# Who makes the low parts of the experts' weights: VectorE with GpSimd, or VectorE alone

## The chip, the cores and the metric

The kernel runs on one core of a Trainium2 chip, in one launch. The metric is the device time of one execution in microseconds; the median of three runs of the kernel before is 1285.52 us (1283.47 to 1285.62). The core has a matrix engine (TensorE, PE in the profile, its weight loads PEld), VectorE (DVE), ScalarE (ACT), GpSimd (POOL) and SyncE (SP), which here only issues the transfers of weights.

## The reference

A two-layer transformer trunk over 256 tokens of 1024 numbers in float32. Each layer is: norm, one projection to 2304 columns, windowed attention on some heads and gated retention on others, an output projection, a residual sum; then norm, a SwiGLU mixer, a residual sum. The mixer of layer 0 is dense, that of layer 1 picks two of eight experts per token:

```python
for l in range(DEPTH):
    h = rms_norm(x, ln_mix[l])
    proj = h @ w_in[l]                                   # 1024 x 2304
    ya, yr = window_sink_attention(...), gated_retention(...)
    x = x + concatenate([ya, yr]) @ w_out[l]             # 1024 x 1024
    h = rms_norm(x, ln_ffn[l])
    if l % 2 == 0: y = swiglu(h, ffn_w_gate, ffn_w_up, ffn_w_down)   # 1024 x 2816, 2816 x 1024
    else:          y = moe_swiglu(h, router_w, exp_w_gate, exp_w_up, exp_w_down)
    x = x + y
# moe_swiglu: for e in 8 experts: y += gates[:, e] * (silu(h @ w_gate[e]) * (h @ w_up[e])) @ w_down[e]
```

## The kernel before

Every weight matrix is streamed once from HBM. The stream is cut into units of 128 x 2048 floats (1 MB), and each unit into two pieces of 128 x 1024. The ring `raw` holds 11 units (`RING`), so 22 pieces. A product in float32 precision is put together from three fast products: each operand is split into a high part (rounded to fp32r) and a low part (the rest). For a weight piece p, ScalarE writes `w_hi` as a rounded copy of the raw piece (`high_part`, line 373, for the pieces ahead of the experts, and `high_part_e`, line 393, for the experts'), and then `w_lo = raw - w_hi` is made (`low_part`, line 382, and `low_part_e`, line 400). `w_hi` has 6 slots (`HIGHS`), `w_lo` 3 (`LOWS`). TensorE's `piece` (line 1142 for every matmul, through `mm`) first does hi x hi and lo x hi with the high part, and only then waits for the low part and does the last third of its matmuls with `w_lo`.

Pieces are numbered through. 118 of them (`FRONT_PIECES`) belong to what comes before the experts: mixing in layer 0 (26), the dense mixer (66), mixing in layer 1 (26, numbers 92 to 117). Then a loop runs over the experts, 8 turns with these inputs (`n_pass` is 1), of 66 pieces each (`FFN_PIECES`): 44 of gate and up together, 22 of down. In `before`, `by_pool(p)` gives each piece with p % 4 == 3 to GpSimd, in front and in the loop alike, and the other three of four to VectorE. Each of the two counts its low parts on a semaphore of its own (`lo_vec`, `lo_pool`).

The order on each engine is written out by hand, and each engine runs its own list in order:
- TensorE: for q in 0..65 the piece q; after q = 5, 9, ... 45 two transposes of the hidden block (line 1139); after q = 3 the eight matmuls that spread the last expert's output over the tokens (`spread_out`); after q = 56 the gather of the next expert's tokens.
- VectorE: low parts 0, 1 and 2 among the low parts of the gathered tokens (line 1047) and of the output (line 1059); then for each q: `add_output` at q = 3 (line 1067, four instructions), at q % 4 == 3 the gated product `hid_e` (line 1105), which waits for ScalarE's silu, which waits for TensorE's piece q; at q % 4 == 1 the low part `heT_lo` of the transposed hidden block (line 1110), which waits for ScalarE's `heT_hi` (line 788); and last, low part q + 3. Low part q + 3 waits until TensorE has used piece q, whose slot it takes.
- ScalarE: for each q its share of the same steps, and last high part q + 6.
- SyncE: the load of unit m waits until the low parts of both pieces of unit m - 11 are made, since it overwrites them (`load_expert`, waits at line 478, loads at 484 and 489).
- GpSimd: in the loop nothing but low parts. Ahead of it, in layer 1's mixing, also the rotary embedding (`rope`, lines 529 to 534).

Of the kernel before, what the change touches and what calls it, by code (L numbers as in the profile page):

```python
# [20 lines left out]
F32 = mybir.dt.float32  # L21
F32R = mybir.dt.float32r
I32 = mybir.dt.int32
ALU = mybir.AluOpType
# [18 lines left out]
N_EXPERTS = 8  # L43
# [7 lines left out]
RING = 11  # L51
HIGHS, LOWS = 6, 3
# [8 lines left out]
FFN_UNITS = GU_UNITS + DOWN_UNITS  # L61
FFN_PIECES = 2 * FFN_UNITS
# [4 lines left out]
FRONT_PIECES = 2 * FRONT_UNITS  # L67
# [16 lines left out]

def by_pool(p):

    return p % 4 == 3


def lows(p, first=0):  # L90

    if p < first:
        done = [-sum(by_pool(q) == b for q in range(p + 1, first)) for b in (False, True)]
    else:
        done = [sum(by_pool(q) == b for q in range(first, p + 1)) for b in (False, True)]
    return done


def constants():
# [55 lines left out]
def trunk(nc, x, ln_mix, w_in, w_out, rel_bias_table, sinks, ln_ffn, ffn_w_gate, ffn_w_up, ffn_w_down,  # L155
          router_w, exp_w_gate, exp_w_up, exp_w_down, ln_final, consts, buckets, out):
    with ExitStack() as ctx:
        def sb(name, shape, dt=F32):
            return ctx.enter_context(nc.sbuf_tensor(name, shape, dt))

        def sem(name):
            return ctx.enter_context(nc.semaphore(name))
# [3 lines left out]
        w_hi = sb("w_hi", [P, HIGHS, PIECE], F32R)  # L166
# [114 lines left out]
        lo_vec, lo_pool = sem("lo_vec"), sem("lo_pool")  # L281
# [57 lines left out]
        for m in range(FFN_UNITS):  # L339
            e_total[e_slot[m]] += 32 if m < GU_UNITS else 16  # L340
            e_landed.append(e_total[e_slot[m]])
        lows_front = lows(FRONT_PIECES - 1)
        lows_e = lows(FFN_PIECES - 1)

        def wait_lows(eng, p, lead=(0, 0), first=0):

            b = by_pool(p)
            eng.wait_ge((lo_vec, lo_pool)[b], lead[b] + lows(p, first)[b])

        assert FRONT_PIECES % 4 == FFN_PIECES % 4 and FFN_UNITS % RING == 0  # L350
        assert FFN_PIECES % HIGHS == 0 and FFN_PIECES % LOWS == 0

        def high_slot(p):
# [6 lines left out]
        def raw_piece(slot, half):  # L360
            return raw[:, slot, half * PIECE:(half + 1) * PIECE]
# [30 lines left out]
            act.wait_ge(piece_used, FFN_PIECES * i + (FRONT_PIECES + q - HIGHS + 1))  # L392
            nc.scalar.activation(w_hi[:, q % HIGHS, :], raw_piece(slot, q % 2), ACT.Copy).then_inc(hi_made, 1)  # L393

        def low_part_e(eng, i, q, pool):
            if q >= FFN_PIECES or by_pool(q) != pool:
                return
            eng.wait_ge(hi_made, FFN_PIECES * i + (FRONT_PIECES + q + 1))
            eng.wait_ge(piece_used, FFN_PIECES * i + (FRONT_PIECES + q - LOWS + 1))
            eng.tensor_tensor(w_lo[:, q % LOWS, :], raw_piece(e_slot[q // 2], q % 2),  # L400
                              w_hi[:, q % HIGHS, :].bitcast(F32), ALU.subtract).then_inc((lo_vec, lo_pool)[pool], 1)

        block = ctx.enter_context(nc.Block())

# [2 lines left out]
        def _(sp):  # L407
# [56 lines left out]
            def load_expert(i, e):  # L464
                for m in range(FFN_UNITS):
                    slot = e_slot[m]
                    freed = []
                    for half in range(2):
                        q = 2 * (m - RING) + half
                        b = by_pool(q % FFN_PIECES)  # L470
                        if q >= 0:
                            rel = lows(q)[b]
                        else:
                            rel = lows(FFN_PIECES + q, FFN_PIECES)[b]
                        freed.append(((lo_vec, lo_pool)[b], sp.to_reg(lows_e[b] * i + (lows_front[b] + rel))))

                    for s, value in freed:
                        sp.wait_ge(s, value)
                    if m < GU_UNITS:
                        j, hf = m // 2, m % 2  # L480
                        dst = raw[:, slot, :].rearrange("p (k g n) -> p k g n", k=4, g=2)
                        for g, w in enumerate((exp_w_gate, exp_w_up)):
                            src = w[0, bass.ds(e, 1), hf * 4 * P:(hf + 1) * 4 * P, j * FC:(j + 1) * FC]
                            sp.dma_start(dst[:, :, g, :], src.rearrange("e (k p) n -> p (e k) n", p=P)).then_inc(raw_landed[slot], 16)
                    else:
                        u = m - GU_UNITS
                        dst = raw[:, slot, :].rearrange("p (k n) -> p k n", k=2)
                        src = exp_w_down[0, bass.ds(e, 1), u * 2 * P:(u + 1) * 2 * P, :]
                        sp.dma_start(dst, src.rearrange("e (k p) n -> p (e k) n", p=P)).then_inc(raw_landed[slot], 16)
# [5 lines left out]
            n = sp.value_load(passes_i[0:1, 0:1], min_val=1, max_val=2)  # L495
# [15 lines left out]
        def _(pool):  # L511
# [28 lines left out]
            first = 0  # L540
# [36 lines left out]
            pool.dma_start(gain[:], ln_final.partition_broadcast(P)).then_inc(gain_landed, 16)  # L577
            pool.wait_ge(route_ready, 1)
            n = pool.value_load(passes_i[0:1, 0:1], min_val=1, max_val=2)
            with pool.Fori(0, n * N_EXPERTS) as i:  # L580
                for q in range(FFN_PIECES):
                    low_part_e(pool, i, q, True)

            pool.wait_ge(gain_landed, 32)
            pool.wait_ge(x_added, n * (4 * N_EXPERTS) + 14)
# [224 lines left out]
        def _(dve):  # L810
# [44 lines left out]
            first = 0  # L855
            for layer in range(DEPTH):
                n = 2 * layer
# [119 lines left out]
                n = 1  # L977
# [67 lines left out]
            def gather_low(i, b):  # L1045
                dve.wait_ge(g_hi, 2 * i + (b + 1))
                dve.tensor_tensor(aT_lo[:, 4 * b:4 * b + 4, 0:P], bank(2 + b).rearrange("p (k t) -> p k t", k=4),
                                  aT_hi[:, 4 * b:4 * b + 4, 0:P].bitcast(F32), ALU.subtract).then_inc(g_lo, 1)

            def rstd_low(i):  # L1050
                dve.wait_ge(rstd_gathered, i + 1)
                dve.tensor_copy(rstd_e[:], psum[:, 5, 300:301]).then_inc(rstd_e_made, 1)
# [35 lines left out]
            dve.wait_ge(route_ready, 1)  # L1088
            n_pass = dve.value_load(passes_i[0:1, 0:1], min_val=1, max_val=2)
            with dve.Fori(0, n_pass * N_EXPERTS) as i:  # L1090
                low_part_e(dve, i, 0, False)
                gather_low(i, 0)
                low_part_e(dve, i, 1, False)
                gather_low(i, 1)
                rstd_low(i)
                for q in range(2, LOWS):
                    low_part_e(dve, i, q, False)
                output_low(i)
                for q in range(FFN_PIECES):
                    j = q // 4  # L1100
                    if q == 3:
                        add_output(i)
                    if q < GU_PIECES and q % 4 == 3:
                        dve.wait_ge(e_gate, NJ * i + (j + 1))
                        dve.scalar_tensor_tensor(out=hid_e[:, j % 2, :], in0=psum[:, j % 2, FC:2 * FC], scalar=rstd_e[:],  # L1105
                                                 in1=hid_e[:, j % 2, :], op0=ALU.mult, op1=ALU.mult).then_inc(e_hid, 1)
                    if q % 4 == 1 and 1 <= j <= NJ:
                        dve.wait_ge(e_hi, NJ * i + j)
                        cols = slice(2 * (j - 1), 2 * j)
                        dve.tensor_tensor(heT_lo[:, cols, :], psum[:, 4 + (j - 1) % 2, 0:256].rearrange("p (k t) -> p k t", k=2),  # L1110
                                          heT_hi[:, cols, :].bitcast(F32), ALU.subtract).then_inc(e_lo, 1)
                    if q == 48:

                        dve.wait_ge(pick_turned, i + 1)
                        mark_slots(i + 1)
                    low_part_e(dve, i, q + LOWS, False)
            turns = n_pass * N_EXPERTS
            output_low(turns)
            add_output(turns)
# [17 lines left out]
        def _(pe):  # L1137
# [24 lines left out]
            def piece(p, products, i=None, each=False, tiles=None):  # L1162

                r = p if i is not None else p - FRONT_PIECES
                high, low = w_hi[:, r % HIGHS, :], w_lo[:, r % LOWS, :]
                if i is None:
                    pe.wait_ge(hi_made, p + 1)  # L1170
                else:
                    pe.wait_ge(hi_made, FFN_PIECES * i + (FRONT_PIECES + p + 1))
                for n, (dst, hi, lo, cols, start, stop) in enumerate(products):
                    if tiles:
                        pe.wait_ge(h_hi, tiles[n])
                        pe.wait_ge(h_lo, tiles[n])
                    mm(dst, hi, high[:, cols], start, False)
                    mm(dst, lo, high[:, cols], False, False)
                if i is None:
                    wait_lows(pe, p)  # L1180
                else:
                    b = by_pool(p)
                    pe.wait_ge((lo_vec, lo_pool)[b], lows_e[b] * i + (lows_front[b] + lows(p)[b]))
                for n, (dst, hi, lo, cols, start, stop) in enumerate(products):
                    ins = mm(dst, hi, low[:, cols], False, stop)
                    if each and n < len(products) - 1:
                        ins.then_inc(product_out, 1)
                ins.then_inc(piece_used, 1)

            pe.wait_ge(i_landed, 16)  # L1190
            first = 0
            for layer in range(DEPTH):
                turn_h(2 * layer)
                for s in range(MIX_PIECES):
                    if s < IN_PIECES:
                        u, half = s // 2, s % 2
# [309 lines left out]
```

## Time and profile before

| what | us |
|---|---|
| median of three runs | 1285.52 |
| span of the profiled execution, first to last instruction | 1282.0 |
| PE matmul busy | 1211.1 (94%) |
| DVE busy | 950.1 (74%) |
| ACT busy | 849.9 (66%) |
| POOL busy | 468.4 (37%) |
| DMA, mean over the span | 268 GB/s |

The profile gives for its own execution the span alone; the median of the runs is 3.5 us above it. The times are inclusive of all stages: the front takes up to about 420 us, the eight turns of the expert loop the rest. Busy shares are means over stages, and a matmul's span overlaps the next one's, so where TensorE loses time is read from the starts of its instructions, not from its busy share. "Idle before" is the time for which an engine stood still ahead of an instruction, and behind the arrow is what it waited for.

### The profile page before, as it was taken

To read this page: it belongs to the slowest core of one execution; us is meant where nothing else is said; L and a number is where in the kernel's file an instruction comes from. 1 tells how busy PE (TensorE), PEld (TensorE's weight loads), DVE (VectorE), ACT (ScalarE), POOL (GpSimd) and SP (SyncE) were. 2 spreads that over 40 slices of the span, in tenths; PEclk is the share of its full clock that TensorE was granted. 3 is DMA by queue.
4 is the path that set the end of the run, shared out by engine and by line. 5 is a ranking of instruction groups with operands and counts; after the bars stand their busy time and mean duration, and the time that the engine had idled before them with its cause. 6 is when DMAs were issued, how large, how long until landed. Compare 5 with 4: busy or idle time off the path is not lost.

```text
span 1282.0 us, 20404 instructions
## 1 busy us (share of the span) xinstructions
PE 1211.1 (94%) x6173; PEld 1001.2 (78%) x6173; DVE 950.1 (74%) x1031; ACT 849.9 (66%) x1108; POOL 468.4 (37%) x204
## 2 busy tenths in 40 slices
PE   7899999999897999999999999999999999999996
PEld 7887888888895877777877777777787777777775
DVE  4765444435766788788788798888978878878885
ACT  6655444435553787677777677778777767768773
POOL 2402211222414254344344444435434534443542
PEclk9999999999998899999999999999999999999999
DMA  9945555565343599999999999999999999999950
GB/s 284 359 134 174 187 197 190 172 191 170 99 150 114 176 349 341 315 329 330 327 322 346 316 315 346 341 301 342 338 316 326 341 316 324 346 341 293 348 197 33
DMA packets 259816, 344.06 MB, mean 268 GB/s; under 512 B 8672, under 2 KB 231088, under 8 KB 259776
## 3 DMA queue, kind: packets, MB, share of 16 engines
q1 hardware_dynamic: 259200, 342.35, 80.4%
q0 software_dynamic: 352, 1.09, 0.3%
q8 instruction: 24, 0.39, 0.1%
q10 hardware_dynamic: 224, 0.10, 0.0%
q14 instruction: 16, 0.13, 0.0%
HBM read 342.06 MB, written 1.44 MB: 268 GB/s over the span
## 4 chain that ended last, share of the span: by engine, by line
PE 67%; DVE 18%; issue 9%; ACT 4%; DMA 2%; DVEq 1%; SPq 0%; ACTq 0%
PE psum L1142 64%; DVE w_lo L400 11%; PE psum L1139 3%; DMA raw<-in_w_in 1%; ACT w_hi L393 1%; DVE x_sb L1067 1%; DVE hid_e L1105 1%; ACT score L666 1%; DVE prob L922 1%; DVE oe_lo L1059 1%; ACT heT_hi L788 1%; ACT aT_hi L758 1%; DVE rt L1020 0%; DVE esink L911 0%; DVE smax L907 0%
## 5 line engine op out<-in xcount | busy, mean ns | idle before, releaser
L400 DVE TENSOR_TENSOR w_lo<-raw,w_hi 128x1024 fp32r<-128x1024 f32 x400 | 599.4, 1528 | 65.5 <-PE psum L1142 63.0
L393 ACT ACTIVATE w_hi<-raw 128x1024 fp32r<-128x1024 f32 x528 | 549.9, 1059 | 131.3 <-PE psum L1142 128.0
L400 POOL TENSOR_TENSOR w_lo<-raw,w_hi 128x1024 fp32r<-128x1024 f32 x128 | 360.8, 2819 | 490.8 <-PE psum L1142 426.1
L1142 PE MATMUL psum<-w_hi,aT_hi 128*128 128x512 f32 (+1 forms) x1232 | 451.6, 375 | 3.3 <-ACT proj L653 2.0
L1142 PE MATMUL psum<-w_hi,aT_lo 128*128 128x512 f32 (+1 forms) x1232 | 442.4, 368 | 0.0
L1142 PE MATMUL psum<-w_lo,aT_hi 128*128 128x512 f32 (+1 forms) x1232 | 326.9, 369 | 25.4 <-DVE w_lo L400 25.4
L1142 PEld LDWEIGHTS psum<-w_lo,aT_hi 128*128 128x128 f32 x1232 | 213.6, 190 | 72.6 <-DVE w_lo L400 35.8
L1142 PEld LDWEIGHTS psum<-w_hi,aT_hi 128*128 128x128 f32 x1232 | 234.3, 190 | 41.4 <-ACT proj L653 2.5
L1142 PEld LDWEIGHTS psum<-w_hi,aT_lo 128*128 128x128 f32 x1232 | 234.3, 190 | 35.0
L373 ACT ACTIVATE w_hi<-raw 128x1024 fp32r<-128x1024 f32 x118 | 124.0, 1058 | 84.0 <-PE psum L1142 75.5
L382 POOL TENSOR_TENSOR w_lo<-raw,w_hi 128x1024 fp32r<-128x1024 f32 x29 | 71.4, 2461 | 260.2 <-PE psum L1142 235.6
L382 DVE TENSOR_TENSOR w_lo<-raw,w_hi 128x1024 fp32r<-128x1024 f32 x89 | 113.4, 1276 | 47.9 <-PE psum L1142 45.9
L1142 PE MATMUL psum<-w_hi,heT_hi 128*128 128x512 f32 x352 | 140.6, 399 | 0.0
L1142 PE MATMUL psum<-w_hi,heT_lo 128*128 128x512 f32 x352 | 139.1, 395 | 0.0
L1142 PE MATMUL psum<-w_lo,heT_hi 128*128 128x512 f32 x352 | 111.6, 398 | 8.8 <-DVE w_lo L400 8.8
L1142 PEld LDWEIGHTS psum<-w_lo,heT_hi 128*128 128x128 f32 x352 | 65.3, 188 | 27.7 <-DVE w_lo L400 12.5
L1110 DVE TENSOR_TENSOR heT_lo<-psum,heT_hi 128x256 fp32r<-128x256 f32 x88 | 36.9, 420 | 61.5 <-ACT heT_hi L788 61.5
L1142 PEld LDWEIGHTS psum<-w_hi,heT_lo 128*128 128x128 f32 x352 | 66.2, 188 | 15.2
L1142 PEld LDWEIGHTS psum<-w_hi,heT_hi 128*128 128x128 f32 x352 | 66.1, 188 | 15.3
L788 ACT ACTIVATE heT_hi<-psum 128x256 fp32r<-128x256 f32 x88 | 33.8, 384 | 47.1 <-PE psum L1139 47.1
L785 ACT ACTIVATE hid_e<-psum,rstd_e 128x256 f32<-128x256 f32 x88 | 41.8, 475 | 28.5 <-PE psum L1142 28.5
L1105 DVE SCALAR_TENSOR_TENSOR hid_e<-psum,rstd_e,hid_e 128x256 f32<-128x256 f32 x88 | 41.9, 476 | 2.7
(188 smaller groups left out, 843.7 us busy)
## 6 DMA issues: line engine op xcount, KB each, us to landing
raw<-in_exp_w_gate SPq DMA_DIRECT2D x176, 512.0 KB, 4.7
raw<-in_exp_w_up SPq DMA_DIRECT2D x176, 512.0 KB, 5.8
raw<-in_exp_w_down SPq DMA_DIRECT2D x88, 1024.0 KB, 6.5
raw<-in_w_in SPq DMA_DIRECT2D x17, 1024.0 KB, 5.4
raw<-in_ffn_w_gate SPq DMA_DIRECT2D x22, 512.0 KB, 4.1
raw<-in_ffn_w_up SPq DMA_DIRECT2D x22, 512.0 KB, 5.1
raw<-in_ffn_w_down SPq DMA_DIRECT2D x11, 1024.0 KB, 4.9
raw<-in_w_out SPq DMA_DIRECT2D x8, 1024.0 KB, 8.0
```

Source lines behind the costliest of these rows:

```text
L373: nc.scalar.activation(high_slot(p), raw_piece((p // 2) % RING, p % 2), ACT.Copy).then_inc(hi_made, 1)
L382: eng.tensor_tensor(low_slot(p), raw_piece((p // 2) % RING, p % 2), high_slot(p).bitcast(F32), ALU.subtract).then_inc((lo_vec, lo_pool)[po ...
L393: nc.scalar.activation(w_hi[:, q % HIGHS, :], raw_piece(slot, q % 2), ACT.Copy).then_inc(hi_made, 1)
L400: eng.tensor_tensor(w_lo[:, q % LOWS, :], raw_piece(e_slot[q // 2], q % 2), w_hi[:, q % HIGHS, :].bitcast(F32), ALU.subtract).then_inc((lo ...
L666: nc.scalar.activation(score[:, c, p, :], score[:, c, p, :], ACT.Exp, bias=nmax[:, col:col + 1], accum_out=psums[:, col:col + 1]).then_inc ...
L758: nc.scalar.activation(aT_hi[:, 4 * b:4 * b + 4, 0:P], bank(2 + b).rearrange("p (k t) -> p k t", k=4), ACT.Copy).then_inc(g_hi, 1)
L785: nc.scalar.activation(hid_e[:, j % 2, :], psum[:, j % 2, 0:FC], ACT.Silu, scale=rstd_e[:]).then_inc(e_gate, 1)
L788: nc.scalar.activation(heT_hi[:, 2 * (j - 1):2 * j, :], psum[:, 4 + (j - 1) % 2, 0:256].rearrange("p (k t) -> p k t", k=2), ACT.Copy).then ...
L1105: dve.scalar_tensor_tensor(out=hid_e[:, j % 2, :], in0=psum[:, j % 2, FC:2 * FC], scalar=rstd_e[:], in1=hid_e[:, j % 2, :], op0=ALU.mult, ...
L1110: dve.tensor_tensor(heT_lo[:, cols, :], psum[:, 4 + (j - 1) % 2, 0:256].rearrange("p (k t) -> p k t", k=2), heT_hi[:, cols, :].bitcast(F32 ...
L1139: return pe.matmul(dst, src, ident, is_transpose=True, start=True, stop=True, skip_group_check=True)
L1142: return pe.matmul(dst, a, b, start=start, stop=stop, skip_group_check=True)
```

## The change

GpSimd makes no low part of an expert's piece any more, nor of the 22 pieces that lie ahead of these in the ring (numbers 96 to 117). VectorE makes them, at the same places of its list by the same rule (low part q + 3 at step q). The other pieces of the front stay divided as they were. With one semaphore for the expert's low parts, the waits of SyncE and of TensorE become simpler: SyncE waits once, for the second piece of the unit, in place of twice. GpSimd's loop over the experts goes.

```diff
 def by_pool(p):
-    return p % 4 == 3
-def lows(p, first=0):
-    ...
+    return p % 4 == 3 and p < FRONT_PIECES - 2 * RING
+def lows(p):
+    return [sum(by_pool(q) == b for q in range(p + 1)) for b in (False, True)]

-        def low_part_e(eng, i, q, pool):
-            if q >= FFN_PIECES or by_pool(q) != pool:
+        def low_part_e(eng, i, q):
+            if q >= FFN_PIECES:
                 return
             eng.wait_ge(hi_made, FFN_PIECES * i + (FRONT_PIECES + q + 1))
             eng.wait_ge(piece_used, FFN_PIECES * i + (FRONT_PIECES + q - LOWS + 1))
             eng.tensor_tensor(w_lo[:, q % LOWS, :], raw_piece(e_slot[q // 2], q % 2),
-                              w_hi[...].bitcast(F32), ALU.subtract).then_inc((lo_vec, lo_pool)[pool], 1)
+                              w_hi[...].bitcast(F32), ALU.subtract).then_inc(lo_vec, 1)

             def load_expert(i, e):
-                    freed = [...]              # one wait for each of the unit's two pieces
-                    for s, value in freed:
-                        sp.wait_ge(s, value)
+                    q = 2 * (m - RING) + 1
+                    sp.wait_ge(lo_vec, FFN_PIECES * i + (lows_front[0] + q + 1))

         # GpSimd
-            with pool.Fori(0, n * N_EXPERTS) as i:
-                for q in range(FFN_PIECES):
-                    low_part_e(pool, i, q, True)

         # VectorE, for each low part of the loop
-                    low_part_e(dve, i, q + LOWS, False)
+                    low_part_e(dve, i, q + LOWS)

         # TensorE, ahead of the last third of a piece
-                    b = by_pool(p)
-                    pe.wait_ge((lo_vec, lo_pool)[b], lows_e[b] * i + (lows_front[b] + lows(p)[b]))
+                    pe.wait_ge(lo_vec, FFN_PIECES * i + (lows_front[0] + p + 1))
```

## Rows read from the trace of the kernel before

**Rows 1.** Waits, whole span: engine and line waited for; us, times, longest us.

```profile
DVE heT_lo L1110 <- ACT heT_hi L788: 61.5, 57, 1.2
...
PE psum L1142 <- DVE w_lo L400: 34.2, 32, 1.4
```

**Rows 2.** The page's part 5: groups (busy, mean ns | idle before, releaser).

```profile
L400 DVE TENSOR_TENSOR w_lo<-raw,w_hi 128x1024 fp32r<-128x1024 f32 x400 | 599.4, 1528 | 65.5 <-PE psum L1142 63.0
...
L400 POOL TENSOR_TENSOR w_lo<-raw,w_hi 128x1024 fp32r<-128x1024 f32 x128 | 360.8, 2819 | 490.8 <-PE psum L1142 426.1
```

**Rows 3.** Line 400: its instructions, ns min/median/max.

```profile
L400 DVE TENSOR_TENSOR w_lo<-raw,w_hi x400: 1204/1214/3447, 419.7 to 1265.7; 128x1024 fp32r<-128x1024 f32 x134
```

**Rows 4.** Timeline of PE, second turn: start us, us, engine, line, what [idle before].

```profile
542.19 0.44 PE L1139 MATMUL psum<-cst,hid_e 128*128 128x128 f32 x2
...
549.17 0.38 PE L1139 MATMUL psum<-cst,hid_e 128*128 128x128 f32 x2
...
560.78 0.38 PE L1139 MATMUL psum<-cst,hid_e 128*128 128x128 f32 x2
...
566.52 0.38 PE L1139 MATMUL psum<-cst,hid_e 128*128 128x128 f32 x2
...
568.94 0.73 PE L1142 MATMUL psum<-w_lo,aT_hi 128*128 128x512 f32 x2 [1.12 <-DVE w_lo L400]
...
570.89 0.39 PE L1142 MATMUL psum<-w_hi,aT_hi 128*128 128x512 f32 x1
...
573.62 0.38 PE L1139 MATMUL psum<-cst,hid_e 128*128 128x128 f32 x2
...
647.43 0.43 PE L1139 MATMUL psum<-cst,hid_e 128*128 128x128 f32 x2
```

**Rows 5.** Timeline of POOL and DVE around that stall.

```profile
565.40 2.40 POOL L400 TENSOR_TENSOR w_lo<-raw,w_hi 128x1024 fp32r<-128x1024 f32 x1 [2.34 <-ACT w_hi L393]
...
565.59 3.29 DVE L400 TENSOR_TENSOR w_lo<-raw,w_hi 128x1024 fp32r<-128x1024 f32 x1
...
568.81 0.41 DVE L1110 TENSOR_TENSOR heT_lo<-psum,heT_hi 128x256 fp32r<-128x256 f32 x1
569.14 2.35 DVE L400 TENSOR_TENSOR w_lo<-raw,w_hi 128x1024 fp32r<-128x1024 f32 x2
571.60 0.48 DVE L1105 SCALAR_TENSOR_TENSOR hid_e<-psum,rstd_e,hid_e 128x256 f32<-128x256 f32 x1
...
574.45 0.42 DVE L1110 TENSOR_TENSOR heT_lo<-psum,heT_hi 128x256 fp32r<-128x256 f32 x1 [1.23 <-ACT heT_hi L788]
```

**Rows 6.** Timeline of PE, same turn, pieces of down.

```profile
603.82 0.48 PE L1142 MATMUL psum<-w_hi,heT_hi 128*128 128x512 f32 x1
...
606.64 0.40 PE L1142 MATMUL psum<-w_hi,heT_hi 128*128 128x512 f32 x1
...
608.04 0.40 PE L1142 MATMUL psum<-w_hi,heT_hi 128*128 128x512 f32 x1
```

**Rows 7.** Windows: stretch, busy by engine, PEclk, DMA share, GB/s.

```profile
30.00:40.00 10.00, 9.29 (x79) 9.09 (x79) 4.40 (x8) 4.92 (x8) 2.31 (x2) 1.00 1.10 348
...
45.00:50.00 5.00, 5.00 (x44) 5.00 (x44) 4.90 (x5) 0.47 (x3) 3.50 (x3) 1.00 1.03 409
...
545.00:650.00 105.00, 100.81 (x465) 81.39 (x464) 89.33 (x84) 79.38 (x95) 45.08 (x16) 1.00 1.00 330
```

**Rows 8.** Timeline of DVE and PE where the second turn begins.

```profile
535.66 3.37 DVE L400 TENSOR_TENSOR w_lo<-raw,w_hi 128x1024 fp32r<-128x1024 f32 x2
...
537.02 0.62 PE L1142 MATMUL psum<-w_lo,aT_hi 128*128 128x512 f32 x2
...
538.95 2.72 DVE L1067 SCALAR_TENSOR_TENSOR x_sb<-psum,gatex,x_sb 128x512 f32<-128x512 f32 x4
```

**Rows 9.** Timeline of PE in layer 1's mixing.

```profile
350.86 3.62 PE L1139 MATMUL psum<-cst,prob 128*128 128x128 f32 x16 [3.22 <-DVE prob L922]
```

**Rows 10.** The page's part 6: loads, count, KB each, median us to landing.

```profile
raw<-in_exp_w_down SPq DMA_DIRECT2D x88, 1024.0 KB, 6.5
```

More of the change, by code:

```diff
@@ L85, in by_pool @@
 def by_pool(p):
-    return p % 4 == 3
-def lows(p, first=0):
[L92 to L96, printed above, removed]
+    return p % 4 == 3 and p < FRONT_PIECES - 2 * RING
+def lows(p):
+    return [sum(by_pool(q) == b for q in range(p + 1)) for b in (False, True)]
 def constants():
@@ L342, in trunk, with wait_lows @@
         lows_front = lows(FRONT_PIECES - 1)
-        lows_e = lows(FFN_PIECES - 1)
-        def wait_lows(eng, p, lead=(0, 0), first=0):
+        def wait_lows(eng, p):
             b = by_pool(p)
-            eng.wait_ge((lo_vec, lo_pool)[b], lead[b] + lows(p, first)[b])
-        assert FRONT_PIECES % 4 == FFN_PIECES % 4 and FFN_UNITS % RING == 0
+            eng.wait_ge((lo_vec, lo_pool)[b], lows(p)[b])
+        assert FFN_UNITS % RING == 0
         assert FFN_PIECES % HIGHS == 0 and FFN_PIECES % LOWS == 0
@@ L400, in low_part_e @@
             eng.tensor_tensor(w_lo[:, q % LOWS, :], raw_piece(e_slot[q // 2], q % 2),
-                              w_hi[:, q % HIGHS, :].bitcast(F32), ALU.subtract).then_inc((lo_vec, lo_pool)[pool], 1)
+                              w_hi[:, q % HIGHS, :].bitcast(F32), ALU.subtract).then_inc(lo_vec, 1)
         block = ctx.enter_context(nc.Block())
@@ L466, in load_expert @@
                     slot = e_slot[m]
[L467 to L475, printed above, removed]
-                    for s, value in freed:
-                        sp.wait_ge(s, value)
+                    q = 2 * (m - RING) + 1
+                    sp.wait_ge(lo_vec, FFN_PIECES * i + (lows_front[0] + q + 1))
                     if m < GU_UNITS:
@@ L1090, in _ @@
             with dve.Fori(0, n_pass * N_EXPERTS) as i:
-                low_part_e(dve, i, 0, False)
+                low_part_e(dve, i, 0)
                 gather_low(i, 0)
-                low_part_e(dve, i, 1, False)
+                low_part_e(dve, i, 1)
                 gather_low(i, 1)
@@ L1096, in _ @@
                 for q in range(2, LOWS):
-                    low_part_e(dve, i, q, False)
+                    low_part_e(dve, i, q)
                 output_low(i)
```

## The prediction

> **What bounds the kernel now.** I read the waits first. TensorE's own waits in the expert loop have one cause: 32 times it stood before the third part of a piece until VectorE had made `w_lo`, 34.2 us by the profile's count [rows 1]. The page's groups show the oddity behind it: the same VectorE instruction takes 1528 ns in the mean but 1214 in the median and 3447 at most [rows 2, 3]. GpSimd takes 2819 ns for the same piece and is idle most of the time [rows 2].
>
> The timeline says what these waits are. Between two pairs of transposes TensorE has four pieces to do, a block. An undisturbed block takes 566.52 - 560.78 = 5.74 us, the next one 573.62 - 566.52 = 7.10, with the wait at 568.94 in it [rows 4]. Beside it [rows 5]: GpSimd starts its low part at 565.40 and needs 2.40; VectorE starts the low part that TensorE wants next at 565.59 and takes 3.29. 1.21 of that is its own time, so it lay still for about 2.1 us, until GpSimd was through at 567.80 (565.40 + 2.40 + 1.09 is 568.89, where VectorE's ends). It is not bandwidth that is shared: one engine waits for the other to end. So each low part given to GpSimd can cost VectorE up to 2.1 us, while making it costs VectorE itself 1.14 (two in a row take 2.35: 2.35 - 1.21 = 1.14 for the second [rows 5]).
>
> **Part 1: GpSimd's 128 low parts of the loop leave.** All 32 waits of TensorE lie in the eight turns, four in each, in the same places: first block, two further blocks of gate and up, one piece of down. What each costs in starts of instructions, which is more than the profile's idle figure since the restart is counted too:
> - first block: 549.17 - 542.19 = 6.98, less 5.74: 1.24 [rows 4];
> - a later block: 7.10 - 5.74 = 1.36, twice a turn [rows 4];
> - in down: 606.64 - 603.82 = 2.82 against 608.04 - 606.64 = 1.40 for a free piece: 1.42 [rows 6].
>
> Sum of a turn 5.38, of eight 43.0 us, if every wait goes and none comes.
>
> **Part 2: VectorE takes over 16 or 17 low parts a turn.** Its busy time in one turn was 89.3 of 105 us (the DVE column of [rows 7]), in which its 50 low parts hold 50 x 1.528 = 76.4. After, 66 x 1.14 to 1.21 = 75.2 to 79.9. So VectorE's load stays about where it is, at 88 to 93 us of a turn of about 100: the lock that goes pays for the work that comes. Whether it is in time is a question of order, and I walk it.
>
> Inside a block (t = 0 at the transposes; TensorE's pieces 1.38 us each, the pair of transposes 0.2; the block's fourth piece back, q % 4 == 3, is used at t = 3.0): ScalarE's half of `heT` lets VectorE start `heT_lo` at t = 0.83 (574.45 - 573.62 [rows 4, 5]). Then 0.33 (569.14 - 568.81), two low parts, 2.3: t = 3.44. The gated product can start 0.71 after the piece is used (571.60 - 570.89 [rows 4, 5]), t = 3.7; 0.4 later the third low part, then the fourth: t = 6.4, and the next `heT_lo` is due at 5.74 + 0.83 = 6.57. So VectorE waits about 0.25 us twice, instead of the 1.23 us once of today [rows 5] (57 waits of mean 1.08 in all [rows 1]), and keeps pace. The piece whose low part is late today gets it at t = 5.3, and TensorE asks for it at 5.74 + 0.13 + 4 x 0.23 = 6.8: 1.5 us to spare. In down nothing but low parts is left, 1.14 against 1.40 a piece.
>
> The start of a turn is the tightest place. VectorE comes out of the output's low part at 535.66 [rows 8]. New there is low part 3, to 536.9; TensorE takes it at 537.02. Then low parts 4 and 5 to 539.1, `add_output` 2.64, the gated product 0.4, low part 6 to 543.3; TensorE's transposes start at 542.19 [rows 4] and its third step of piece 6 at about 543.25. Low parts 7 and 8 then have 0.1 to 0.2 us to spare, and from there the spare grows. Against this stands that VectorE's list ahead of 535.66 starts some tenths earlier too, since GpSimd's part is out of its way. I take 0.15 us lost a turn, 1 us in all; ends: 0, and the 1.24 of today coming back each turn, 10 us.
>
> **Part 3: the front.** Five pieces move (99, 103, 107, 111, 115). Above: all on the path, 5 x 1.14 = 5.7 us more. Below: TensorE's one wait there for VectorE, 3.22 us for the attention weights [rows 9]; GpSimd works beside these on the rotary embedding, which stays where it is, so this wait should stay too. The new low parts fall where VectorE waits for TensorE or where TensorE has pieces in hand. I take 0, ends -3.2 and +5.7.
>
> **Part 4: SyncE waits once per unit instead of twice, TensorE on one semaphore.** The second piece's low part comes after the first's on VectorE, so nothing is released earlier or later by it; SyncE's list has no other work, and loads run 22 pieces ahead. Taken as 0; the bound on either side is under 1 us for the whole loop, for the first load alone would show it.
>
> **Part 5: transfers.** A turn brings 33 units of 1.05 MB, 34.6 MB. It takes 647.43 - 542.19 = 105.24 us now [rows 4], 329 GB/s (330 in the window, with a DMA share of 1.00 [rows 7]). At 99.9 us it must be 346. Where loads were free to run, early in the kernel, the rate was 348 with rows of 1 KB and 409 in a window with output weights, whose rows are 4 KB [rows 7], as the down weights' are. 22 units at 348 and 11 at 409 take 66.3 + 28.2 = 94.5 us; all at 348, 99.4. So transfers just fit, and the ring of 11 units evens out the stretches.
> The Trainium skill, DMA: Bandwidth & Descriptors, section Specifications, gives about 358 GB/s as the limit of a core's share of HBM. By that rule a turn could not go under an estimated 34.6 MB / 358 = 96.6 us: of the 5.38 us a turn that I count, none is refused, but 3.3 us more would be all that any further gain could bring. The 409 of the trace lies above the rule's figure, so the trace does not bear it out for rows of 4 KB.
>
> **Sum.** 1282.0 - 43.0 + 1 = 1240.0 us of span. The execution profiled has its span alone on record; the median of the runs is 3.5 above, which I take to be what lies around the span and leave as it is: 1243.5 us.
>
> **The rivals.**
> - *The start of a turn stays late* (0.12). VectorE's list of 535 to 546 is a chain without slack; if each low part there takes its 1.21 instead of 1.14 and a wake-up more, one wait a turn stays, 8 x 1.24 = 10 us, up to two: 1253 to 1262. For it: the spare of 0.1 us. Against: three waits of four lie elsewhere.
> - *The transfers become the bound* (0.10). The share of 1.00 at 330 GB/s can mean that the engines are full now. If the rate stops at 340, a turn takes 101.8, 15 us more than forecast: 1259. Against: a unit of the down weights lands 6.5 us after its issue [rows 10], and the ring has it issued 22 pieces, some 31 us, ahead of its use, so there is no long queue today. If the rate stopped at 330 nothing would be gained, the next case.
> - *The change doesn't do what it says: no gain* (0.03). Either the transfers as above, or the long VectorE instructions are not GpSimd's doing and stay: 1282 to 1288. The times of start and end above speak against it.
> - *Slower* (0.04). VectorE's list is in order, and GpSimd's low parts did not stand behind the waits for ScalarE. If VectorE still waited 1.23 us for `heT_hi` in each block, a block would be 4 x 1.14 + 0.33 + 0.4 + 1.23 = 6.52 us, against a mean now of 5.74 + (1.24 + 2 x 1.36)/11 = 6.10: 0.42 x 11 x 8 = 37 us more, 1322. It decides from a remaining wait of 6.10 - 5.29 = 0.81 us a block on. Against: that wait is there because VectorE comes early, having three low parts to make; with four it comes when ScalarE is done.
> - *The forecast* (0.71), own range 1239 to 1249.
>
> **How the numbers follow.** A difference under 0.2% (2.6 us) is what a measurement of this kernel can't tell from none. Faster: the forecast, the first two rivals, 0.93. Same: 0.03. Slower: 0.04. The range goes to 1258: it takes in part of the late start and of the transfers; below, to 1237, for the front's 3.2 us and a block a little under 5.74. That leaves out less than 2 in 10.
>
> **What would show it.** Right: VectorE's low parts all near 1214 ns with a maximum under 1.3 us in the loop; turns 99.9 us apart; no wait of TensorE for `w_lo` beyond the first block; mean wait for `heT_hi` at 0.3 us; the window rate at 346 GB/s with landings still under 8 us. Wrong: waits of TensorE at pieces 3, 6, 7 or 8 of each turn (late start); waits of ScalarE's high parts for transfers (transfers); waits for `heT_hi` over 0.81 us with TensorE waiting behind them (slower).

## The result and the profile after

| | before | after |
|---|---|---|
| median, us | 1284.49 of 4 executions (1282.99 to 1285.62) | 1235.64 of 4 (1233.91 to 1236.50) |
| ratio | 1 | 0.9619 [0.9605, 0.9633] |
| span of the profiled execution | 1282.0 | 1232.1 (own time 1233.91) |

The kernel is 3.8% faster, 48.9 us. I had forecast 1243.5 with a range of 1237 to 1258: the direction and most of the size are right, but the time lies 7.9 us below the forecast and 1.4 us below the range. The span shows the same 7.9: 1240.0 was forecast, 1232.1 came.

The page of the kernel after, busy time by engine and the groups of low parts (line 395 is the loop, 377 the front); they answer to [rows 2]:

```profile
PE 1197.1 (97%) x6173; PEld 1001.4 (81%) x6173; DVE 965.1 (78%) x1164; ACT 849.5 (69%) x1108; POOL 94.9 (8%) x71
...
L395 DVE TENSOR_TENSOR w_lo<-raw,w_hi 128x1024 fp32r<-128x1024 f32 x528 | 625.9, 1218 | 52.6 <-PE psum L1124 49.7
...
L377 POOL TENSOR_TENSOR w_lo<-raw,w_hi 128x1024 fp32r<-128x1024 f32 x24 | 58.6, 2443 | 221.1 <-PE psum L1124 202.9
```

VectorE makes 528 low parts in 625.9 us, where 400 had taken 599.4 [rows 2]: 128 more for 26.5 us. The durations of single instructions (ns min/median/max) show why, beside [rows 3]:

```profile
L395 DVE TENSOR_TENSOR w_lo<-raw,w_hi x528: 1202/1217/1228, 415.2 to 1215.2; 128x1024 fp32r<-128x1024 f32 x176
L377 DVE TENSOR_TENSOR w_lo<-raw,w_hi x94: 1207/1219/3387, 11.4 to 387.3; 128x1024 fp32r<-128x1024 f32 x94
```

In the loop the maximum is 1228 ns instead of 3447. In the front, where GpSimd still works, 3387 is still there. TensorE's waits, the whole list, against [rows 1] (engine and line waited for; us, times, longest us):

```profile
PE psum L1121 <- DMA x_sb<-in_x: 6.6, 2, 5.1
PE psum L1124 <- DVE mask L1010: 6.6, 1, 6.6
PE psum L1121 <- DVE prob L904: 5.7, 2, 3.2
PE psum L1124 <- DVE oe_lo L1041: 1.5, 1, 1.5
PE psum L1121 <- DVE probT L909: 1.3, 1, 1.3
PE psum L1124 <- ACT proj L635: 1.0, 1, 1.0
PE psum L1124 <- DVE pick L1025: 1.0, 1, 1.0
PE psum L1124 <- ACT w_hi L368: 0.6, 1, 0.6
PE psum L1124 <- DVE lgT L985: 0.6, 1, 0.6
```

No wait for `w_lo` is left, where there were 32. The transposes that begin the blocks, TensorE's timeline, against [rows 4]:

```profile
482.44 0.38 PE L1121 MATMUL psum<-cst,hid_e 128*128 128x128 f32 x2
...
488.25 0.38 PE L1121 MATMUL psum<-cst,hid_e 128*128 128x128 f32 x2
...
530.53 0.38 PE L1121 MATMUL psum<-cst,hid_e 128*128 128x128 f32 x2
...
536.23 0.38 PE L1121 MATMUL psum<-cst,hid_e 128*128 128x128 f32 x2
...
588.06 0.38 PE L1121 MATMUL psum<-cst,hid_e 128*128 128x128 f32 x2
```

The last block of one turn begins at 488.25, that of the next at 588.06: a turn is 99.81 us, within 0.01 the same in all of them, against 105.24 in the turn of [rows 4]. The stretch from its last block over down to the next turn's first transposes (488.25 to 530.53) takes 42.28. The first block (530.53 to 536.23) takes 5.70, where it took 6.98; most of the later ones take 5.73.

And VectorE across one block, the counterpart of [rows 5]:

```profile
480.83 2.35 DVE L395 TENSOR_TENSOR w_lo<-raw,w_hi 128x1024 fp32r<-128x1024 f32 x2
483.27 0.42 DVE L1092 TENSOR_TENSOR heT_lo<-psum,heT_hi 128x256 fp32r<-128x256 f32 x1
483.62 2.35 DVE L395 TENSOR_TENSOR w_lo<-raw,w_hi 128x1024 fp32r<-128x1024 f32 x2
486.16 0.48 DVE L1087 SCALAR_TENSOR_TENSOR hid_e<-psum,rstd_e,hid_e 128x256 f32<-128x256 f32 x1 [0.19 <-ACT hid_e L767]
486.56 2.35 DVE L395 TENSOR_TENSOR w_lo<-raw,w_hi 128x1024 fp32r<-128x1024 f32 x2
489.08 0.42 DVE L1092 TENSOR_TENSOR heT_lo<-psum,heT_hi 128x256 fp32r<-128x256 f32 x1 [0.17 <-ACT heT_hi L770]
```

Four low parts stand in each block and the only waits are two of under 0.2 us, as walked. (This is the last block of a turn, 5.81 us long; in most blocks the second wait is 0.10.) `heT_hi` was made 1.23 us too late for VectorE before [rows 5]; now VectorE comes 1.2 us later and hardly waits. The same stretch as in [rows 7], and the landings beside [rows 10]:

```profile
545.00:650.00 105.00, 105.00 (x489) 86.28 (x488) 96.01 (x105) 83.65 (x102) 0.00 (x0) 1.00 1.03 347
```

```profile
raw<-in_exp_w_gate SPq DMA_DIRECT2D x176, 512.0 KB, 4.7
raw<-in_exp_w_up SPq DMA_DIRECT2D x176, 512.0 KB, 5.7
raw<-in_exp_w_down SPq DMA_DIRECT2D x88, 1024.0 KB, 6.0
```

TensorE fills the whole window, loads run at 347 GB/s, and a down unit lands no later than before (6.0 us against 6.5). The transfers are no bound.

**Where the 49.9 us of span came from.** I cut both traces at the first pair of `hid_e` transposes, 436.82 before and 430.80 after. Behind the cut: 1282.0 - 436.82 = 845.2 and 1232.1 - 430.80 = 801.3, so the loop with its end gave 43.9. Ahead of it: 6.0, in the front, for which I had forecast nothing. Of these, 0.7 lie ahead of layer 1's `rstd`, where nothing was changed: single executions differ there by up to 3.8 us (the same `esink` of layer 0 starts between 45.3 and 49.1). From `rstd` on it is 5.3. Its first part is plain once one looks at small instructions. Kernel before, VectorE and then GpSimd, in the softmax of layer 1:

```profile
334.94 0.17 DVE L910 TENSOR_TENSOR smax<-smax,sinkc 128x16 f32<-128x16 f32 x1
335.15 2.30 DVE L911 TENSOR_TENSOR esink<-sinkc,smax 128x16 f32<-128x16 f32 x1
```

```profile
335.02 2.40 POOL L382 TENSOR_TENSOR w_lo<-raw,w_hi 128x1024 fp32r<-128x1024 f32 x1 [0.68 <-PE psum L1142]
```

Kernel after, VectorE at the same place:

```profile
334.12 0.17 DVE L892 TENSOR_TENSOR smax<-smax,sinkc 128x16 f32<-128x16 f32 x1
334.33 0.17 DVE L893 TENSOR_TENSOR esink<-sinkc,smax 128x16 f32<-128x16 f32 x1
...
341.67 6.26 DVE L904 TENSOR_TENSOR prob<-score,rden 128x256 f32<-128x256 f32 x8
```

A subtraction of 16 columns took 2.30 us while GpSimd made the low part of piece 103, and takes 0.17 without. It stands on the chain from the scores to TensorE. Next, TensorE's transposes of the attention weights, after, beside [rows 9]; and the window 340 to 360 of both kernels, before first:

```profile
347.98 1.97 PE L1121 MATMUL psum<-cst,prob 128*128 128x128 f32 x16 [2.44 <-DVE prob L904]
```

```profile
340.00:360.00 20.00, 15.75 (x119) 15.35 (x118) 15.19 (x19) 12.66 (x35) 8.19 (x9) 0.91 0.39 122
```

```profile
340.00:360.00 20.00, 17.56 (x194) 17.09 (x193) 15.21 (x20) 10.66 (x20) 6.37 (x9) 1.00 0.46 140
```

Before, TensorE stood 3.22 us for the weights, and its granted clock was 0.91 in the stretch, so for part of it at the lower level of 1.2 GHz; the sixteen transposes took 3.62 us. After, it stood 2.44 us and the clock was 1.00, all of it at 2.4 GHz: 1.97 us. The shorter wait is no gain beside the 2.2 us (from the start of `nmax` to the first transpose it is 13.4 us in both). Nor is it shown to be what keeps the clock. In layer 0 of the kernel before, the same transposes stand behind a wait of the same length and are fast:

```profile
62.69 1.96 PE L1139 MATMUL psum<-cst,prob 128*128 128x128 f32 x16 [3.22 <-DVE prob L922]
```

A larger victim of the same kind was left standing. In layer 1's routing GpSimd makes the low parts of the tokens while VectorE picks each token's second expert. Kernel after, the timeline of both:

```profile
403.39 2.34 POOL L559 TENSOR_TENSOR aT_hi<-xg,xg_hi 128x1024 fp32r<-128x1024 f32 x1 [1.35 <-ACT xg_hi L730]
403.60 4.46 DVE L1002 SCALAR_TENSOR_TENSOR rt<-rt,rc,cst 128x8 f32<-128x8 f32 x2
...
405.70 2.33 POOL L559 TENSOR_TENSOR aT_lo<-xg,xg_hi 128x1024 fp32r<-128x1024 f32 x1
```

Two instructions of eight columns take 4.46 us; their like on the first expert, with nothing beside them on GpSimd, take 0.36. They stand on the chain to the mask, for which TensorE waits 6.6 us, its longest wait for VectorE. So it is in every run here, the kernel before included; up to 4.1 us may lie in it, an estimate (4.46 - 0.36) that no run tried.

### The profile page after: what moved, and what is told of

Read it like the earlier page. It is cut to its first block, busy times and chain, and to the rows that moved or that the text cites. A ratio compares the mean times of both kernels' runs of the same rounds, so it can differ in the third digit from the quotient of the medians.

```text
span 1232.1 us, 19788 instructions
## 1 busy us (share of the span) xinstructions
PE 1197.1 (97%) x6173; PEld 1001.4 (81%) x6173; DVE 965.1 (78%) x1164; ACT 849.5 (69%) x1108; POOL 94.9 (8%) x71
## 4 chain that ended last, share of the span: by engine, by line
PE 94%; DVE 3%; ACT 1%; issue 1%; DMA 1%; SPq 0%; DVEq 0%; ACTq 0%
PE psum L1124 90%; PE psum L1121 3%; ACT score L648 1%; DVE prob L904 1%; DMA raw<-in_w_in 1%; DVE rt L1002 0%; DVE smax L889 0%; DVE w_lo L377 0%; DVE esink L893 0%; DVE x_sb L831 0%; DVE score L886 0%; DVE x_sb L1049 0%; ACT w_hi L368 0%; DVE aT_lo L818 0%; SPq L418 0%
## 5 line engine op out<-in xcount | busy, mean ns | idle before, releaser
L395 DVE TENSOR_TENSOR w_lo<-raw,w_hi 128x1024 fp32r<-128x1024 f32 x528 | 625.9, 1218 | 52.6 <-PE psum L1124 49.7
L1124 PE MATMUL psum<-w_lo,aT_hi 128*128 128x512 f32 (+1 forms) x1232 | 323.0, 366 | 0.0
L377 DVE TENSOR_TENSOR w_lo<-raw,w_hi 128x1024 fp32r<-128x1024 f32 x94 | 117.4, 1252 | 48.4 <-PE psum L1124 47.0
L377 POOL TENSOR_TENSOR w_lo<-raw,w_hi 128x1024 fp32r<-128x1024 f32 x24 | 58.6, 2443 | 221.1 <-PE psum L1124 202.9
```

The costliest lines, as they stand in the source:

```text
L377: eng.tensor_tensor(low_slot(p), raw_piece((p // 2) % RING, p % 2), high_slot(p).bitcast(F32), ALU.subtract).then_inc((lo_vec, lo_pool)[po ...
L1124: return pe.matmul(dst, a, b, start=start, stop=stop, skip_group_check=True)
```

## The experiments

The theory after the result: the lock between VectorE and GpSimd is the one cause, and it acts in two places, 43.9 us in the loop and some 4 us in the front. The rivals: the gain is something else of the change (fewer waits of SyncE, fewer instructions), GpSimd blocks by any work and not by reading, or the front's share is chance.

**Loop and front apart.** `by_pool` and the front's waits, kernel after to experiment; SyncE's first turn is written out so that it waits for both engines:

```diff
 def by_pool(p):                      # the front only; the loop stays as after
-    return p % 4 == 3 and p < FRONT_PIECES - 2 * RING
+    return p % 4 == 3
```

> The change in the expert loop alone; the five pieces ahead of it stay on GpSimd. Theory (the loop's 32 waits of TensorE were worth 43.4 us, as the transposes in the two traces say, and the five pieces of layer 1's mixing the other 5 to 6): 1284.5 - 43.4 = 1241 us, ratio 0.966. Rival (the front's share is chance between two executions, and the loop is worth all 49): 1236 us, the same as the changed kernel.

1240.18 us (1237.77 to 1242.05, 5 executions), ratio 0.9647 [0.9634, 0.9660], span 1240.2. No wait for `w_lo` in the loop, and 801.2 us behind the cut, against 801.3 in the kernel after. All that is missing is in the front: 4.5 us by the medians, 3.6 by the ratios.

The converse: only the five front pieces moved, the loop's low parts divided as before. `by_pool_front` takes the place of `by_pool` in the front's low parts and in the waits for them; SyncE's first turn is again written out.

```diff
-def by_pool(p):
-    return p % 4 == 3 and p < FRONT_PIECES - 2 * RING
+def by_pool(p):                      # the expert loop, as before
+    return p % 4 == 3
+def by_pool_front(p):
+    return p % 4 == 3 and p < FRONT_PIECES - 2 * RING
```

> The five pieces ahead of the loop alone move to VectorE; in the loop GpSimd keeps its share. Theory: 5 to 6 us faster than before, 1279 us, ratio 0.996, and the 32 waits of the loop stay. Rival (the front is worth nothing, as the prediction had it): 1284.5, ratio 1.000.

1281.20 us (1278.33 to 1282.72, 5), ratio 0.9965 [0.9952, 0.9979]: 4.5 us by the ratio (2.7 to 6.2 by its interval). The loop's waits stand as they were, the list of TensorE's waits headed by

```profile
PE psum L1157 <- DVE w_lo L410: 35.3, 32, 1.4
```

So each half brings its part alone: 0.9647 x 0.9965 = 0.9613, against 0.9619 for both. "The front is worth nothing" falls.

**Which piece of the front.** Only piece 103 goes back to GpSimd; SyncE's first turn waits for both engines, as above.

```diff
 def by_pool(p):
-    return p % 4 == 3 and p < FRONT_PIECES - 2 * RING
+    return p % 4 == 3 and (p < FRONT_PIECES - 2 * RING or p == 103)
```

> The changed kernel with one piece, number 103, back on GpSimd. Theory (the front's sure gain is this piece alone: its low part on GpSimd held VectorE's 16-column esink subtraction at 2.30 us where it takes 0.17, on the chain that leads to the attention weights; the rest of the front's gain is TensorE's clock behind it): esink back at 2.30, front as before, 1240 us, ratio 0.965. Rival (the other four pieces matter too): 1236 to 1238.

1239.40 us (1238.19 to 1240.11, 5), ratio 0.9654 [0.9641, 0.9667], 4.5 us over the kernel after by the ratios. VectorE's short subtraction is long again:

```profile
335.12 2.30 DVE L898 TENSOR_TENSOR esink<-sinkc,smax 128x16 f32<-128x16 f32 x1
```

The whole gain of the front hangs on piece 103; the other four pieces, 1.14 us of VectorE each, cost and bring nothing that can be told apart.

**Is it the reading?** The kernel after, and GpSimd does again, at the moments of its old low parts, a subtraction of the same size on constants that nobody reads. The first form reads and writes 1024 columns; the second subtracts one column and fills 1279 with zeros.

```diff
+            spare = cst[:, C_DEC:C_DEC + 1280]
+            with pool.Fori(0, n * N_EXPERTS) as i:
+                for k, q in enumerate(range(3, FFN_PIECES, 4)):
+                    ...              # the two waits of the old low part, and one for GpSimd's own last instruction
+                    pool.tensor_tensor(spare[:, 0:PIECE], spare[:, 0:PIECE], spare[:, 0:PIECE], ALU.subtract)...
```

> The changed kernel, and GpSimd in the loop runs a subtraction of 128x1024 floats of its own, on data that nobody uses, at the moments at which it had made its low parts. Theory (GpSimd's reads lock VectorE's low parts out for as long as they last): each of 16 a turn costs VectorE up to 2.1 us on top of its 88 us a turn; at 1.7 in the mean a turn takes 88 + 27 = 115 us and the kernel some 120 us more than the changed one, 1355 us; at the least the 32 waits come back, 1279. Rival (the waits came from GpSimd's own 2.8 us for a piece, not from what it does to VectorE): 1236, unchanged.

1337.75 us (1337.13 to 1338.38, 2), ratio 1.0411 [1.0392, 1.0430]. The groups of 545 to 1200 us:

```profile
L395 DVE TENSOR_TENSOR w_lo<-raw,w_hi 128x1024 fp32r<-128x1024 f32 x384 | 566.1, 1515 | 11.8 <-PE psum L1131 11.8
L571 POOL TENSOR_TENSOR cst<-cst 128x1024 f32<-128x1024 f32 x94 | 208.3, 2216 | 448.8 <-ACT w_hi L388 316.3 <-PE psum L1131 132.5
```

and one case of it, the timeline of GpSimd, VectorE and TensorE:

```profile
598.92 1.89 POOL L571 TENSOR_TENSOR cst<-cst 128x1024 f32<-128x1024 f32 x1 [4.77 <-ACT w_hi L388]
...
599.29 3.74 DVE L395 TENSOR_TENSOR w_lo<-raw,w_hi 128x1024 fp32r<-128x1024 f32 x2
...
601.95 0.73 PE L1131 MATMUL psum<-w_lo,aT_hi 128*128 128x512 f32 x2 [0.67 <-DVE w_lo L395]
```

Two low parts take 3.74 us in place of 2.35. GpSimd began at 598.92 and was through at 600.81; 3.74 - 2.35 = 1.39, and 600.81 - 599.29 = 1.52. It is slower than the kernel before by 4.1%, since here VectorE has all low parts to make and is held up as well: it has no wait left in its blocks, and TensorE waits 109 times for `w_lo`, 65.8 us. I had expected some 17 us more: the subtraction that reads one buffer twice took 1.89 us in the median and not 2.40, so each lock was shorter. The rest of the change, the simpler waits of SyncE and TensorE, is in this run too and doesn't save it; what they are worth by themselves no run shows.

```diff
-                    pool.tensor_tensor(spare[:, 0:PIECE], ...)
+                    pool.tensor_tensor(spare[:, 0:1], spare[:, 0:1], spare[:, 0:1], ALU.subtract)...
+                    pool.memset(spare[:, 1:640], 0.0)...
+                    pool.memset(spare[:, 640:1280], 0.0)...
```

> As the one before, but GpSimd fills memory with zeros (1279 columns in two pieces, about 1.4 us by the 0.30 us of its 256 columns in the trace), behind a subtraction of one column. If only GpSimd's reads lock VectorE out, VectorE's low parts keep 1.21 us and the kernel its 1236. If any use of its path does, each costs VectorE up to 1.2 us, 88 + 16 x 0.9 = 102 us a turn, 1255 or more. The Trainium skill, SBUF - State Buffer, section Who interferes with whom, has a VectorE instruction with two SBUF inputs contend with GpSimd's reads, not with one that only writes: by it 1236.

1236.31 us (1235.84 to 1236.78, 2), ratio 0.9621 [0.9604, 0.9639]: the kernel after. Groups of the same stretch:

```profile
L395 DVE TENSOR_TENSOR w_lo<-raw,w_hi 128x1024 fp32r<-128x1024 f32 x437 | 518.0, 1218 | 38.8 <-PE psum L1133 37.8
...
L573 POOL MEMSET cst<- 128x640 f32 x106 | 67.0, 632 | 0.0
```

VectorE's mean stays at 1218 ns beside the fills. It is an instruction of GpSimd that reads (and writes) that holds VectorE's two-input instruction; being busy and writing are not enough. One that only reads was not run. This is what the Trainium skill says (SBUF — State Buffer, section Who interferes with whom): a VectorE instruction with two inputs in SBUF contends with a GpSimd instruction that reads SBUF, not with one that only writes it. Both halves of the rule agree with these two runs, 1515 and 1218 ns.

**How much room VectorE has.** The kernel after, with a fill of a spare buffer on VectorE in each block of gate and up, of 512 columns and then of 1024.

```diff
                     low_part_e(dve, i, q + LOWS)
+                    if q < GU_PIECES and q % 4 == 2:
+                        dve.memset(cst[:, C_DEC:C_DEC + 512], 0.0)      # second run: 1024
```

> The changed kernel with one more instruction on VectorE in each of the 88 blocks of gate and up, a fill of 512 columns (0.51 us in the trace), its result unused. It asks how much time VectorE has left. Theory (a block takes 5.73 us and VectorE's work in it 4 x 1.14 + 0.33 + 0.4 = 5.3, so 0.4 to 0.5 us are free): the addition is hidden but for at most 0.1 us a block, 1236 to 1245 us. Rival (the waits for ScalarE are fixed and the order leaves nothing free): 88 x 0.5 = 44 us more, 1280.

1237.49 us (1236.52 to 1238.30, 4), ratio 0.9637 [0.9621, 0.9654]; the blocks stayed at 5.73 and VectorE's two waits a block went. The fill takes 485 ns, from its start to the next one's 0.41, and the gated product behind it 0.28 in place of 0.40, now that it doesn't wait for ScalarE: 0.29 us more a block, and free there. It isn't quite free at the start of a turn, the tightest place of the walk: the stretch from the last block to the next turn's first transposes grew from 42.28 to 42.57, and a turn from 99.81 to 100.13.

> The same with a fill of 1024 columns, about 1.0 us. Theory: VectorE's work in a block becomes 5.3 + 1.0 = 6.3 us and is now the bound: 0.57 us a block more, 88 x 0.57 = 50 us, 1286 us, and the gain of the change is gone. Rival (VectorE runs ahead in down and the slots of w_lo hide it): under 1250, which three slots can't do by this theory.

1279.76 us (1276.63 to 1281.52, 8), ratio 0.9966 [0.9954, 0.9978]: nearly the whole gain is gone. The fill takes 912 ns, 0.83 from start to start: 0.71 us more a block. TensorE's timeline:

```profile
560.46 0.44 PE L1123 MATMUL psum<-cst,hid_e 128*128 128x128 f32 x2 [0.29 <-DVE hid_e L1087]
...
566.68 0.44 PE L1123 MATMUL psum<-cst,hid_e 128*128 128x128 f32 x2 [0.25 <-DVE hid_e L1087]
...
572.90 0.44 PE L1123 MATMUL psum<-cst,hid_e 128*128 128x128 f32 x2 [0.25 <-DVE hid_e L1087]
```

A block is 6.22 us now, and 88 x (6.22 - 5.73) = 43 us. TensorE waits for the gated product, the last thing of VectorE's list in a block. The sum fits within 0.1: of the 5.73 us of most blocks VectorE waited 0.19 + 0.10 = 0.29, so its list is 5.44 long, and 5.44 + 0.71 is 6.15. After the change TensorE is the bound, with VectorE 0.29 us a block (5%) behind it.

**Could more be had?** No low part on GpSimd at all:

```diff
 def by_pool(p):
-    return p % 4 == 3 and p < FRONT_PIECES - 2 * RING
+    return False
```

> GpSimd makes no low part at all, layer 0 included. Theory: the same 2.1 us of esink go in layer 0, and with the shorter wait the transposes of the attention weights may keep the full clock, 1.6 us more: 2.2 to 4 us below the changed kernel, 1232 to 1233.5. Rival (VectorE, which then makes all of layer 0's and the dense mixer's low parts as well, becomes late there): 1236 or more, with waits of TensorE for w_lo in the dense mixer.

1233.70 us (1232.88 to 1234.72, 5), ratio 0.9608 [0.9595, 0.9622]. The `esink` of layer 0 went from 2.30 to 0.18 us as well, and from there to the `esink` of layer 1 it takes 286.4 us, against 288.2 to 288.4 in the eleven other profiled executions of kernels that keep it on GpSimd: 1.8 us. But in the times the two intervals overlap: a gain over the kernel after isn't shown, nor the 2 us ruled out.

The attention weights themselves are locked by GpSimd's rotary embedding. Here that waits until they are made (on top of the last experiment):

```diff
                     if s == 9:
+                        pool.wait_ge(prob_ready, 8 * (layer + 1))
                         rope(layer, 1)
```

> As the one before, and GpSimd starts the second part of the rotary embedding only when VectorE has made the attention weights (8 instructions, 6.2 us beside GpSimd's work). Theory (these are held by the same lock): they take about 8 x 0.35 = 2.8 us, TensorE's wait of 2.4 us for them goes in both layers, 4.9 us below the one before, 1228. Rival (the embedding is then late for TensorE's transposes of it, which come some 5 us behind): a wait there takes back half or all, 1230 to 1233.

1233.80 us (1230.48 to 1235.65, 5), ratio 0.9611 [0.9595, 0.9627]: no gain over the last. VectorE's eight products, here and, in the second fence, without the wait:

```profile
339.02 2.77 DVE L905 TENSOR_TENSOR prob<-score,rden 128x256 f32<-128x256 f32 x8
```

```profile
341.03 6.24 DVE L904 TENSOR_TENSOR prob<-score,rden 128x256 f32<-128x256 f32 x8
```

The lock is gone, 3.5 us, and TensorE then waits for what GpSimd makes later:

```profile
PE psum L1122 <- POOL proj L519: 4.5, 2, 2.2
```

A gain turned into a new wait.

**The same kernels once more,** for how much of the front is chance: the kernel after and the kernel before, one profiled execution each.

> The changed kernel once more, for its timeline. Sure by the theory: esink 0.17 us, turns of 99.8 us. Chance by the theory: whether TensorE keeps its full clock over the transposes of the attention weights (1.97 us or over 3) and when it comes back behind the routing (22.1 to 23.6 us from the mask matmuls to the first transposes of the loop).

> The kernel before once more. If the wait of 3.2 us always costs the clock and one of 2.4 only sometimes: transposes over 3 us and 23.6 us again.

1238.02 and 1281.98 us, spans 1236.2 and 1280.2. Behind the cut this pair differs by 44.3 us (845.35 and 801.04). Up to the cut the kernel before is even 0.4 quicker here (434.8 and 435.2), since it reached the `rstd` of layer 1 by chance 3.8 us sooner. The table takes the front of layer 1 apart in all profiled executions but that of the later rotary part, where other waits stand (us; from the timelines of VectorE and TensorE): from the start of the reciprocal that begins `rstd` to the start of `nmax`, which holds `esink`; the wait for the attention weights, and their transposes; from the routing mask's matmuls to the first `hid_e` transposes; and the whole from `rstd` to these.

| kernel | rstd to nmax | wait | transposes | mask to hid_e | rstd to hid_e |
|---|---|---|---|---|---|
| before | 27.40 | 3.22 | 3.62 | 23.58 | 126.73 |
| before, again | 27.42 | 3.20 | 3.28 | 23.32 | 126.26 |
| loop alone | 27.40 | 3.21 | 3.63 | 23.61 | 126.75 |
| 103 back | 27.29 | 3.23 | 3.56 | 23.63 | 126.70 |
| after | 25.16 | 2.44 | 1.97 | 22.07 | 121.42 |
| after, again | 25.17 | 2.45 | 1.96 | 23.46 | 122.84 |
| front alone | 25.17 | 2.44 | 3.11 | 22.28 | 123.24 |
| reads added | 25.18 | 2.45 | 2.63 | 22.54 | 123.45 |
| fills added | 25.17 | 2.44 | 1.97 | 23.64 | 122.98 |
| VectorE +0.49 | 25.17 | 2.45 | 1.97 | 22.08 | 121.47 |
| VectorE +0.91 | 25.18 | 2.45 | 1.97 | 22.32 | 121.71 |
| all on VectorE | 25.27 | 2.47 | 3.42 | 22.12 | 123.22 |

The first column is sure: 2.2 us, in every execution, by piece 103 alone. The transposes are a matter of TensorE's clock: after a wait of 3.2 us they took 3.28 to 3.63 every time, after one of 2.4 us between 2.63 and 3.42 in three of eight, and 1.97 in five. That looks like a rule, and layer 0 doesn't bear it out: behind its wait of 3.2 us, which stands in eleven of these executions, the same transposes took 1.97 us in six and 2.41 to 3.51 in five, and behind the 2.47 us of the twelfth 3.63. So that the change buys the faster clock isn't shown. The column from the mask falls to 22.1 to 22.5 in six of the eight, and never without the change. It follows the moment at which the clock comes back to 2.4 GHz, 13 to 14 us behind the mask's matmuls in these six and 15.7 to 16.3 in the others; what decides that in one execution stays open. The whole is 126.6 us in the mean without the change in the front and 122.5 with it: 4.1 us, which fits the 3.6 to 4.5 of the times better than the 6.0 of the two profiles.

## Why the prediction was right in the loop and wrong in the front

- *What bounds the kernel, and the lock*: right. The cause of the 32 waits was GpSimd's reading, shown by the two runs with reads and with fills.
- *Part 1 and the turn start*: 43.0 us were counted and 1 taken off, 42.0; 43.9 came. No wait is left at the start of a turn, so the 1 us wasn't lost. The other 0.9 is that I read one turn, 105.24, where the seven between first transposes took 105.32 in the mean, and that they take 99.80 instead of 99.86. The run with the loop alone measures this part by itself: 801.2 us behind the cut.
- *Part 2, VectorE's load and order*: right. Its list is as walked, 91 us a turn (96.01 of 105 in the window), and it has 0.29 us a block to spare (0.5 were in the walk).
- *Part 3, the front*: the step that failed. I took 0, with -3.2 as the lower end; the comparisons of several executions show 3.6 to 4.5 us gained, and the two profiles 6.0, of which 0.7 is no part of the change. I had asked which of TensorE's waits for VectorE GpSimd's low parts stretch, found the 3.22 us of [rows 9], saw that the rotary embedding is what stands beside it, and stopped. The lower end was the whole of that wait; but a chain can shrink ahead of the wait that ends it. The lock is held by GpSimd's instruction, so its price doesn't go with the size of the victim: 2.1 us for 16 columns. I had this rule from the loop (3.29 us for 1.21) and applied it only to instructions of 1024 columns. For TensorE's clock I had no term at all. It gave 1.6 us at the transposes and 1.5 behind the mask between the two profiles, but not in every execution, and what brings it stays open.
- *Part 4, SyncE*: nothing to see in it, and none of the 7.9 us is left for it. It wasn't tried by itself.
- *Part 5, transfers*: right. 347 GB/s against 346 needed, landings not longer.
- *Around the span*: I left the 3.5 us between the profiled span and the median as they were. After, they are 1235.64 - 1232.1 = 3.5 again: 1.8 lie around the span of that execution, and 1.7 are there because it was the quickest of its four. For the kernel before the split isn't on record.

The 7.9 us in one line, for the spans: 6.0 ahead of the cut, 0.7 of it by chance, and 1.9 loop. For the median, the front is 3.6 to 4.5 of it, the loop 1.9, and the kernel before came out 1.0 lower in the comparison than in the runs I started from; 0.5 to 1.4 is left to the difference between executions. None of the rivals came: no late start of a turn, no bound by transfers, and the wait for `heT_hi`, on which the slower case hung, is under 0.2 us.

## What to carry to other kernels

When work leaves GpSimd, list every VectorE instruction with two inputs in SBUF that overlapped with it, the tiny ones first, and ask of each whether it stands on a chain that TensorE waits for: what it loses is the rest of GpSimd's instruction, whatever its own size. It can pay to move work to the engine that is busier if the lock costs that engine more than the work does (here 2.1 us against 1.14), but walk its list block by block to see that it keeps pace. Where a part is costed at nothing, the lower end must be what its whole chain can shrink by, not the length of its last wait.

## What the runs showed that I had not expected

- A VectorE subtraction of 16 columns took 2.30 us beside a GpSimd instruction of 2.40, and 0.17 without it. Two VectorE instructions of 8 columns took 4.46 us beside two of GpSimd, in a row, of 2.34.
- It goes both ways: in the run with fills GpSimd's subtraction of one column took 0.18 us at the least and 0.69 in the median, with VectorE's low parts beside it.
- TensorE's clock isn't the same from one execution to the next at the same place: behind the same wait of 3.2 us in layer 0, the same sixteen transposes took 1.97 us in six executions and 2.41 to 3.51 in five.
- The weights' loads ran at up to 391 GB/s in a fortieth of the span (31 us) in the kernel after and no instruction of the loop waited for them. That is over the figure of 358 that I had weighed; the Trainium skill, HBM Reference, section Specifications (TRN2), says that a core which streams alone goes above its share, and with one core at work this trace agrees.
- A fill on GpSimd costs VectorE nothing, 1218 ns beside it and without it.
